# Up projections of the MLPs: high and low half of the input past one weight block as one product of 512 columns

## The reference, cut to what matters

```python
D_MODEL, SEQ, D_FF = 1024, 256, 4 * 1024

def squared_relu_mlp(h, w1, w2):          # w1: 1024 x 4096, w2: 4096 x 1024
    return jnp.square(jax.nn.relu(h @ w1)) @ w2
```

## Time and profile before

| | us |
|---|---|
| median of 3 runs | 1525.03 (1524.64 to 1530.78) |
| the profiled execution, its own time | 1525.93 |
| its span, first to last instruction | 1523.9 |
| TensorE busy with products | 1357.9 (89%) |
| VectorE busy | 1044.0 (69%) |
| ScalarE busy | 598.5 (39%) |
| mean granted TensorE clock | 0.952 of full |

### The profile page before, as it was taken

One profiled execution on the slowest core, in us unless ns is written; L12 is line 12 of the kernel. 1 busy time (PEld: TensorE's weight loads), 2 busy tenths in 40 slices (PEclk: granted clock), 3 DMA queues, 4 the chain that ended last, 5 costly groups with the idle time before them and its releaser, 6 DMA issues.

```text
span 1523.9 us, 22456 instructions
## 1 busy us (share of the span) xinstructions
PE 1357.9 (89%) x8718; PEld 1206.9 (79%) x8718; DVE 1044.0 (69%) x1478; ACT 598.5 (39%) x800; POOL 2.9 (0%) x5
## 2 busy tenths in 40 slices
PE   3875889999898788999959997999996899999997
PEld 3753679999797677999849986899986676899996
DVE  6979788777777757766676785755568645575554
ACT  1424333343344424333345322534336453353332
POOL 0000000000000000000000000000000000000000
PEclk9898889999899998999979998999999999999999
DMA  9653438877375334655516430455452310454540
GB/s 357 262 184 106 153 116 328 315 268 257 122 266 185 132 111 181 231 215 191 203 48 224 139 111 28 166 193 191 171 189 107 135 63 29 166 208 175 188 160 28
DMA packets 45841, 262.90 MB, mean 173 GB/s; under 512 B 5191, under 2 KB 6855, under 8 KB 21066
## 3 DMA queue, kind: packets, MB, share of 16 engines
q1 hardware_dynamic: 32672, 216.88, 39.2%
q10 hardware_dynamic: 13102, 45.09, 8.5%
HBM read 260.90 MB, written 1.05 MB: 172 GB/s over the span
## 4 chain that ended last, share of the span: by engine, by line
PE 73%; DVE 17%; ACT 4%; issue 3%; DMA 2%; ACTq 0%; DVEq 0%; SPq 0%
PE banks L530 21%; PE banks L531 21%; PE banks L532 21%; DVE w_lo L1496 3%; DMA A<-ada_w 2%; PE banks L737 2%; PE banks L998 2%; PE banks L694 1%; ACT A L1053 1%; ACT w_hi L1037 1%; DVE A L1516 1%; DVE hT_lo L1485 1%; PE banks L640 1%; DVE A L1505 1%; DVE mx L1602 1%
## 5 line engine op out<-in xcount | busy, mean ns | idle before, releaser
L1496 DVE TENSOR_TENSOR w_lo<-raw,w_hi 128x2048 fp32r<-128x2048 f32 x193 | 439.8, 2287 | 160.4 <-ACT w_hi L1037 158.1
L1037 ACT ACTIVATE w_hi<-raw 128x2048 fp32r<-128x2048 f32 x193 | 368.8, 1913 | 246.4 <-PE banks L532 211.6
L530 PE MATMUL banks<-hT_hi,w_hi 128*128 128x256 f32 x1432 | 414.0, 289 | 7.6 <-DVE hT_lo L1485 3.3
L532 PE MATMUL banks<-hT_hi,w_lo 128*128 128x256 f32 x1432 | 410.2, 286 | 0.0
L531 PE MATMUL banks<-hT_lo,w_hi 128*128 128x256 f32 x1432 | 410.1, 286 | 0.0
L530 PEld LDWEIGHTS banks<-hT_hi,w_hi 128*128 128x128 f32 x1432 | 280.2, 196 | 13.5 <-issue 7.4
L531 PEld LDWEIGHTS banks<-hT_lo,w_hi 128*128 128x128 f32 x1432 | 280.1, 196 | 3.3 <-issue 1.0
L532 PEld LDWEIGHTS banks<-hT_hi,w_lo 128*128 128x128 f32 x1432 | 279.7, 195 | 0.0
L530 PE MATMUL banks<-w_hi,R 128*128 128x512 f32 (+1 forms) x592 | 231.2, 390 | 3.9 <-DVE R L1485 3.6
L531 PE MATMUL banks<-w_lo,R 128*128 128x512 f32 (+1 forms) x592 | 229.3, 387 | 0.0
L532 PE MATMUL banks<-w_hi,R 128*128 128x512 f32 (+1 forms) x592 | 228.7, 386 | 0.0
(11 more groups left out here) (221 smaller groups left out, 1329.1 us busy)
## 6 DMA issues: line engine op xcount, KB each, us to landing
raw<-stream SPq DMA_DIRECT2D x193, 1024.0 KB, 4.8
A<-ada_w ACTq DMA_DIRECT2D x73, 512.0 KB, 5.4
A<-ada_w SPq DMA_DIRECT2D x16, 512.0 KB, 9.8
A<-ln_g ACTq DMA_DIRECT2D x4, 512.0 KB, 4.0
A<-ln_b ACTq DMA_DIRECT2D x4, 512.0 KB, 5.5
A<-ada_w SPq DMA_DIRECT2D x1, 1536.0 KB
A<-x_t SPq DMA_DIRECT2D x2, 512.0 KB, 12.4
X<-ada_w SPq DMA_DIRECT2D x1, 1024.0 KB
```

The source lines that it names most:

```text
L530: pe.matmul(o, lh, rh, start=start, stop=False, skip_group_check=True)
L532: return pe.matmul(o, ll, rh, start=False, stop=stop, skip_group_check=True)
L1037: act.activation(w_hi[:, s, :], raw[:, s, :], ACT.Copy).then_inc(hi_done, 1)
L1496: v.tensor_tensor(w_lo[:, s, :], raw[:, s, :], w_hi[:, s, :], ALU.subtract).then_inc(lo_done, 1)
```

## The change

`hT_hi` and `hT_lo` become the two halves of one tensor `hT` (128 x 2 x 8 x 256). In `up`, the first two products of `mm3` become one of 512 columns, whose moving operand is hT_hi and hT_lo of the tile kt (two runs of 256 floats, 2048 floats apart); the third, with w_lo, stays. Each column half a has a bank of its own now: high times high and low-weight times high add up in its columns 0 to 255, high-weight times low in 256 to 511. A pair so holds two banks (2kp and 2kp+1), and the four banks 0 to 3 serve two pairs.

ScalarE copies columns 256 to 511 of both banks to `u_f`, without Relu. VectorE adds columns 0 to 255 from PSUM (new, raising the new semaphore `u_sum`), then one scalar_tensor_tensor computes max(u, 0) * u in the place of the squaring. The bank is free when `u_sum` is raised. The gate rows move from banks 2 and 3 to 0 and 1 and wait for `u_sum` of pair 14.

```diff
--- before.py
+++ after.py
@@ -104,8 +104,8 @@
         w_hi = sb("w_hi", [P, SLOTS, UNIT], f32r)
         w_lo = sb("w_lo", [P, SLOTS, UNIT], f32r)
         X = sb("X", [P, TT, D])
-        hT_hi = sb("hT_hi", [P, KT, SEQ], f32r)
-        hT_lo = sb("hT_lo", [P, KT, SEQ], f32r)
+        hT = sb("hT", [P, 2, KT, SEQ], f32r)
+        hT_hi, hT_lo = hT[:, 0], hT[:, 1]
         R = sb("R", [P, 2, KT, SEQ], f32r)
         A = sb("A", [P, ARENA])
         ident = sb("ident", [P, P])
@@ -221,6 +221,7 @@
          n_ready, pair_turned, pair_f, pair_ready, x_ready) = map(sem, (
             "hi_done", "lo_done", "unit_done", "fill_done", "fill_read", "u_ready", "v_step", "y_done", "y_read",
             "rstd_ready", "n_ready", "pair_turned", "pair_f", "pair_ready", "x_ready"))
+        u_sum = sem("u_sum")
         ld_xt = [sem(f"ld_xt{i}") for i in range(2)]
         ld_late = [sem(f"ld_late{i}") for i in range(2)]
         late_used, late_bias, late_zero = map(sem, ("late_used", "late_bias", "late_zero"))
@@ -763,26 +764,30 @@
                 f0, p0 = n["fill"], n["plain"]
 
                 def up(k, kp, u, s):
-                    if isinstance(k, int) and k < 2:
-                        claim((f0 + kp) % 2)
-                    else:
-                        pe.wait_ge(fill_read, k + (p0 - 1))
+                    first = isinstance(k, int) and k < 2
+                    if not first:
+                        pe.wait_ge(u_sum, k + (PAIRS * m - 1))
                     pe.wait_ge(lo_done, u + 1)
                     wh = w_hi[:, s, :].rearrange("p (k n) -> p k n", k=KT)
                     wl = w_lo[:, s, :].rearrange("p (k n) -> p k n", k=KT)
                     late = isinstance(k, int) and k == 0 and m >= 2
-                    order = [(a, kt) for a in range(2) for kt in range(KT)]
+                    sides = (f0 % 2, 1 - f0 % 2)
+                    order = [(a, kt) for a in sides for kt in range(KT)]
                     if late:
-                        order = [(a, kt) for half in range(2) for a in range(2) for kt in range(4 * half, 4 * half + 4)]
+                        order = [(a, kt) for half in range(2) for a in sides for kt in range(4 * half, 4 * half + 4)]
                     for a, kt in order:
-                        if isinstance(k, int) and k == 0 and a == 0 and kt % 4 == 0:
+                        bank = B[2 * kp + a]
+                        if first and kt == 0:
+                            claim(2 * kp + a)
+                        if isinstance(k, int) and k == 0 and a == sides[0] and kt % 4 == 0:
                             pe.wait_ge(pair_ready, n["pair"] - (0 if kt else 1))
-                        if late and (a, kt) == (1, 0):
+                        if late and (a, kt) == (sides[1], 0):
                             group_x(2, 1, 1, True)
                             n["y"] += 2 * TT
-                        last = mm3(B[(f0 + kp) % 2][:, 256 * a:256 * a + 256],
-                                   wh[:, kt, P * a:P * a + P], wl[:, kt, P * a:P * a + P],
-                                   hT_hi[:, kt, :], hT_lo[:, kt, :], kt == 0 and not (late and a), kt == KT - 1)
+                        pe.matmul(two(bank), wh[:, kt, P * a:P * a + P], hT[:, :, kt, :], start=kt == 0, stop=False,
+                                  skip_group_check=True)
+                        last = pe.matmul(bank[:, 0:256], wl[:, kt, P * a:P * a + P], hT_hi[:, kt, :], start=False,
+                                         stop=kt == KT - 1, skip_group_check=True)
                     last.then_inc(unit_done, 1)
 
                 def dn(k, kp, u, s, first=False):
@@ -807,19 +812,19 @@
                 up(k, k % 2, T_unit(u0, k), T_unit(u0, k) % SLOTS)
                 if s_gate:
                     pe.wait_ge(late_used, KT * (m + 1))
+                    pe.wait_ge(u_sum, PAIRS * (m + 1) - 1)
                     for h in range(2):
-                        mm = pe.matmul(B[2 + h][:, :], ones[:, :], gate_r[:, 512 * h:512 * h + 512], start=True, stop=True)
+                        mm = pe.matmul(B[h][:, :], ones[:, :], gate_r[:, 512 * h:512 * h + 512], start=True, stop=True)
                     mm.then_inc(gate_ps, 1)
                     n["gates"] += 1
-                    held[3] = (gate_read, n["gates"])
                 weights(D_unit(u0, k))
                 pe.wait_ge(u_ready, PAIRS * m + k)
                 down_last(D_unit(u0, k - 1), [(u_hi[j], u_lo[j]) for j in ((k - 1) % 2, k % 2)],
                           lambda: pe.wait_ge(u_ready, PAIRS * m + k + 1))
                 n["fill"] += PAIRS
                 n["plain"] += PAIRS
-                for j in range(2):
-                    held[(f0 + j) % 2] = (fill_read, n["plain"] - 1 + j)
+                for b in range(4):
+                    held[b] = (gate_read, n["gates"]) if s_gate and b < 2 else (u_sum, PAIRS * (m + 1) - 1 + b // 2)
 
             def gate(first=False):
 
@@ -1125,7 +1130,7 @@
                     act.wait_ge(unit_done, u + 1)
                     if not (isinstance(k, int) and PAIRS * m + k < 2):
                         act.wait_ge(u_ready, k + (PAIRS * m - 1))
-                    act.activation(u_f[:, kp, :], B[(f0 + kp) % 2][:, :], ACT.Relu).then_inc(fill_read, 1)
+                    act.activation(two(u_f[:, kp, :]), banks[:, 2 * kp:2 * kp + 2, 256:512], ACT.Copy).then_inc(fill_read, 1)
 
                 relu(0, 0, T_unit(u0, 0))
                 ahead(T_unit(u0, 0))
@@ -1158,7 +1163,7 @@
                             for part in range(SUMS[s_ada]):
                                 load_ada(s_ada, KT - 1, part)
                 if s_gate:
-                    gate_rows(2)
+                    gate_rows(0)
                 n["fill"] += PAIRS
 
             def gate_rows(b):
@@ -1531,7 +1536,11 @@
 
                 def square(k, kp, step, u_free):
                     v.wait_ge(fill_read, k + (p0 + 1))
-                    v.tensor_tensor(u_f[:, kp, :], u_f[:, kp, :], u_f[:, kp, :], ALU.mult).then_inc(v_step, 1)
+                    v.tensor_tensor(two(u_f[:, kp, :]), banks[:, 2 * kp:2 * kp + 2, 0:256], two(u_f[:, kp, :]),
+                                    ALU.add).then_inc(u_sum, 1)
+                    v.wait_ge(u_sum, k + (PAIRS * m + 1))
+                    v.scalar_tensor_tensor(out=u_f[:, kp, :], in0=u_f[:, kp, :], scalar=0.0, in1=u_f[:, kp, :],
+                                           op0=ALU.max, op1=ALU.mult).then_inc(v_step, 1)
                     v.wait_ge(v_step, step + 1)
                     if u_free is not None:
                         v.wait_ge(unit_done, u_free + 1)
```

## The result

The changed kernel takes 1529.2 us (median of 20 runs, 1524.3 to 1534.1), the kernel before 1526.2 beside it (20 runs). The ratio is 1.0021, 95% interval 1.0011 to 1.0030: some 3 us slower, where 8.4 us less were forecast. The profiled execution has a span of 1530.3 us.

What follows compares the result with a forecast made beforehand. TensorE was taken to bound the MLPs. A gain of 11.8 us there less 3.4 us lost to VectorE's addition made -8.4 us, from 1525.03 to 1516.6 us; its own range 1513 to 1520, with rivals 1511 to 1530.

Steps and rivals of the forecast that it cites:

- Now they are 227.5 + 120.0 = 347.5 ns.: TensorE time per group (one a, one kt) in up: one 512-column and one 256-column product, 12.5 ns less than 360.0.
- the 11.8: TensorE's forecast gain in us over the four MLPs: 944 of 1024 groups, 12.5 ns saved in each.
- rivals 1 and 3: Two-run operand of the merged product: costs two starts, 240.0 ns, 1528.4 us (chance 0.18); or more, 253.3 ns, 1541.0 us (0.09).
- Rival 4: Merged product in up hides what surrounds it and takes 213.3 ns, a larger gain: 1503.2 us; chance 0.06.
- Rival 2: In up, the long-short pair keeps most of the 12.5 ns; a fifth is saved, 2.4 us, giving 1526.0; chance 0.07.
- Loss: 1.44 + 1.44 + 0.54 = 3.4 us.: VectorE's added 0.72 us per pair, unhidden at starts of M0 and M1, ends of M2 and M3, and end of M0.
- The stretch behind M3: End of M3, where u of pair 15 is already late: 0.72 us more, TensorE's wait growing to 0.8.
- the starts: Starts of M0 and M1, where dn(0) already waits for VectorE: 2 x 0.72 = 1.44 us lost.
- No wait for w_lo or u_lo may appear inside the loop of M0.: Check on M0: VectorE's added work stays hidden in the loop, so TensorE never waits there for these low parts.
- The cycle sum of 19.1 of 22.04 us: VectorE's work in M0 per two pairs, 17.7 us plus 1.4 more, claimed to stay below TensorE's 22.04 us.
- the stretches at half clock move by a microsecond or two: Uncertainty from half-clock stretches when the order shifts; one reason for the forecast's own range of 1513 to 1520 us.

Runs made afterwards that it cites:

- eights: Changed kernel with each column half's eight long (512-column) products ahead of its eight short (256-column) ones; ratio to the kernel before 0.9988.
- clean start: Residual gain and bias moved ahead of pair 14, sums cleared after pair 0, modulation loads a unit earlier; ratio 1.0001 in the changed kernel, 1.0000 in the one before.
- taken apart: Changed kernel with clean start, its 512-column product split again into two of 256; banks, copy and addition kept; 1532.0 us, ratio 1.0034.
- Fours: Changed kernel with four long (512-column) products, then four short (256-column) ones, within each run of four kt; ratio to the kernel before 0.9992.

## Why the prediction was wrong

- **"Now they are 227.5 + 120.0 = 347.5 ns."** The step that failed in the TensorE part. The 227.5 was read where long products follow long ones, the 120.0 where short ones follow short ones, and the change alternates them. Mixed so, they cost 352.9 ns. 944 x 5.4 = 5.1 us of the 11.8. In eights, with a pair of changes for each column half, the pair is 11.018 us, as worked out. The Trainium skill, "TensorE: Matmul & The Clock Gate", section "Wait — 56ns, not 53.3ns?", has about 2.5 ns beside the columns; the eights save 1024 products in all and the pair falls by 11.212 - 11.018 = 0.194 us, 16 products of 12.1 ns. The measurement decides, and it is not 2.5 ns here.
- **The jump between two runs** (rivals 1 and 3, 0.27 of the chances) costs nothing: 11.099 us with it and without. Rival 4 didn't come either. Rival 2 named the right place, "kept by the pair of one long and one short product", with a wrong size: 7 of the 12.5 ns are saved, not 2.5.
- **"Loss: 1.44 + 1.44 + 0.54 = 3.4 us."** The second step that failed, and a mis-sized term. Four pairs of runs price the addition: 6.3 us in the kernel before, 6.1 or 4.0 in the changed one (by its first or second ratio), 5.2 twice with the starts moved. The stretch behind M3 was right (0.72 for 0.72, with a wait of 0.58 where 0.8 was said). For the starts I added 0.72 to the waits of one profile: dn(0) was to wait 0.9 us in M0 and 1.3 in M1, and waits 2.3 and 2.0. What I left out is that TensorE may arrive earlier (2 us in M0, by the clock alone), that the sums ahead of pair 2's u hang on loads, and that a late end of M2 is followed by more half clock up to M3 (2.7 and 5.3 us longer in the two profiles of the changed kernel, of which 0.7 was counted).
- **"No wait for w_lo or u_lo may appear inside the loop of M0."** It appeared at dn(2), 2.4 us. The cycle sum of 19.1 of 22.04 us held from pair 3 on, but not for pair 2, whose turn on VectorE hangs on a DMA. What makes that DMA late is open.
- **The clock outside the MLPs was counted at next to nothing** ("the stretches at half clock move by a microsecond or two"). All timed runs give 0.950 for the kernel before and 0.9465 for the changed one. That is 152 and 163 us at half clock. The Trainium skill, "TensorE: Matmul & The Clock Gate", section "HAM oscillation — how this bites in real kernels", puts the loss at half of such time: for 11 us more an estimate of 5.5 us as the most, if TensorE alone counted there. The traces show less where other engines set the pace: without the addition and with a clean start the clock is 0.91 in the first 40 us behind M2 (1.00 with the products of before), and M2 to M3 is only 0.3 us longer. So how much of the loss is the clock's was not measured.
- **Right:** TensorE bounds M2 and M3 wholly (busy for the whole stretch, 161.1 us of 161.1), the copy, the scalar_tensor_tensor and the banks cost nothing in the loops (taken apart, with all of them, the pair is at 11.212 us again), the gate rows wait for nothing, dn(0) of M2 and M3 doesn't wait for u_lo, VectorE is not the bound.

The sum, from the runs: -7.2 us by the pair (64 x 0.113), of which the whole shows 5.0 with clean starts (within the intervals) and about 3 with the starts as changed (1.0041 to 1.0021, and 1.0000 to 0.9981); +4 to +6 us by the addition. That is -1 to +3 us, and the two measurements of the changed kernel gave +1 and +3.

Open is why a late end of M2 brings a stretch at half clock 156 us later. The runs show that this stretch goes with the added operation (12 of 13 profiles with it, none of 5 without) and not with the form of the product, and that 0.6 us is the only wait that is new at the end of M2; no run varies that wait alone.

The eights with the clean start take 1520.7 us beside 1527.2 (0.9958, 0.9944 to 0.9973) and beat both kernels.

## What to carry to other kernels

Take the step of a product from a row where its neighbours have the width that they will have; when two widths are mixed, group them. An operation added to a chain that an engine waits for is not priced by its length alone: look at what the wait releases late, and try it alone in the old kernel. When the part made faster is faster and the whole is not, compare the mean granted clock over all runs, and then look where the half clock lies: where TensorE waits for others anyway it costs little.

## What was not expected of the hardware

- A product of 512 columns followed by one of 256: 235.7 ns from start to start; 256 followed by 512: 117.2. In runs of a kind: 227.8 and 119.9. So the alternation costs 5.2 ns a group. Fours win back only part of it (pair 11.066 us), eights all (11.018).
- A moving operand of two runs, 8 KB apart, costs as much as one run: pair 11.099 us in both.
- With the same instructions and 0.6 us more of waiting ahead of them, the stretch from M2 to M3 has 13.7 us at half clock in place of 3.4 (the kernel before with and without one operation more). The last 3.4 us of it cost 1.5 us, the rest, where waits of TensorE for VectorE got shorter, 0.5. The stretch's length told the kernels with VectorE's added operation from those without in 17 of 18 profiles.
